# An MoE decoder step on one core: the experts' half tiles move between the raw weights, and they and the weights to rounder addresses

## The reference

```python
def expert_block(args):
    xb, e = args                      # 128 gathered rows, one expert
    hid = jax.nn.silu(xb @ w_gate[e]) * (xb @ w_up[e])
    return hid @ w_down[e]            # 1024 -> 512 -> 1024

yb = lax.map(expert_block, (x_pad, block_e)).reshape(P, D)
```

## The kernel before

| tile | start before | mod 256 |
|---|---|---|
| `raw` (gate, up, down, 16,384 bytes each) | 58,176 | 64 |
| `wh` | 107,328 | 64 |
| `wl` | 156,480 | 64 |
| `xg` | 205,792 | 224 |
| `xh`, `xl` | 209,888 and 213,984 | 224 |
| `hid`, `hh`, `hl` | 218,080, 220,128 and 222,176 | 224 |
| `y` | 224,224 | 224 |

## Time and profile before

### The profile page before, as it was taken

How to read it: one execution, slowest core, us unless ns; L and a number is a source line. 1 busy time by engine, 2 the same in 40 slices (tenths; PEclk the granted TensorE clock), 3 DMA queues, 4 the chain that set the end, 5 groups by cost and what they waited for, 6 DMA issues and landing times. The chain is left out here.

```text
span 2469.8 us, 39160 instructions
## 1 busy us (share of the span) xinstructions
PE 2251.6 (91%) x11590; PEld 1673.2 (68%) x11590; DVE 1330.9 (54%) x2251; ACT 1097.6 (44%) x1870; POOL 326.6 (13%) x387
## 2 busy tenths in 40 slices
PE   7999997889689999999799999999989599999974
PEld 4766665667578888887486565656577488888851
DVE  4223212586766656663683443433367677755757
ACT  3221212642346655663443343434332266645645
POOL 0000002660011111010100433000000010100103
PEclk8999998999889999999899999999999699999987
DMA  7566655655558777785456544333261388866956
GB/s 281 175 209 218 224 190 166 188 178 197 177 206 296 274 251 278 275 292 178 143 169 203 183 147 139 94 103 102 90 214 43 134 319 317 315 230 222 321 196 225
DMA packets 194323, 503.98 MB, mean 204 GB/s; under 512 B 19152, under 2 KB 39089, under 8 KB 187696
## 3 DMA queue, kind: packets, MB, share of 16 engines
q1 hardware_dynamic: 165902, 409.88, 49.0%
q0 software_dynamic: 18416, 64.11, 7.5%
q10 hardware_dynamic: 9906, 28.75, 3.1%
HBM read 437.13 MB, written 73.42 MB: 207 GB/s over the span
## 5 line engine op out<-in xcount | busy, mean ns | idle before, releaser
L2260 DVE TENSOR_TENSOR e_wl<-e_raw,e_wh 128x1024 fp32r<-128x1024 f32 x384 | 452.2, 1221 | 117.2 <-ACT e_wh L2168 116.6
L2168 ACT CAST e_wh<-e_raw 128x1024 fp32r<-128x1024 f32 x384 | 379.4, 1048 | 84.7 <-DMA e_raw<-in_e_up 29.1
L2080 PE MATMUL e_psG<-e_wh,e_xh 128*128 128x512 f32 x784 | 320.5, 409 | 11.5 <-issue 7.4
L2082 PE MATMUL e_psG<-e_wh,e_xl 128*128 128x512 f32 x784 | 310.5, 396 | 0.0
L2081 PE MATMUL e_psG<-e_wl,e_xh 128*128 128x512 f32 x784 | 308.9, 394 | 0.0
L2080 PEld LDWEIGHTS e_psG<-e_wh,e_xh 128*128 128x128 f32 x784 | 147.8, 189 | 45.1 <-issue 12.9
L2082 PEld LDWEIGHTS e_psG<-e_wh,e_xl 128*128 128x128 f32 x784 | 147.4, 188 | 36.8
L2081 PEld LDWEIGHTS e_psG<-e_wl,e_xh 128*128 128x128 f32 x784 | 148.1, 189 | 31.4
L615 PE MATMUL in_ps<-in_w_upper,in_h_upper 128*128 128x512 f32 x384 | 155.3, 404 | 3.3 <-DVE in_h_lower L335 2.9
L2080 PE MATMUL e_psY<-e_wh,e_hh 128*128 128x512 f32 x392 | 155.6, 397 | 2.8 <-DVE e_hl L2283 2.8
L2082 PE MATMUL e_psY<-e_wh,e_hl 128*128 128x512 f32 x392 | 157.1, 401 | 0.0
(11 more groups left out here) (614 smaller groups left out, 4359.1 us busy)
## 6 DMA issues: line engine op xcount, KB each, us to landing
e_raw<-in_e_gate SPq DMA_DIRECT2D x32, 2048.0 KB, 11.7
e_raw<-in_e_up SPq DMA_DIRECT2D x32, 2048.0 KB, 9.1
e_raw<-in_e_down SPq DMA_DIRECT2D x32, 2048.0 KB, 8.1
x<-in_ada_w SPq DMA_DIRECT2D x40, 1024.0 KB, 5.3
yrows<-e_y ACTq DMA_DIRECT2D x49, 512.0 KB, 6.3
x<-in_cache SPq DMA_DIRECT2D x64, 320.0 KB
a_pages<-in_cache SPq DMA_DIRECT2D x64, 320.0 KB, 3.5
qkvo<-in_out SPq DMA_DIRECT2D x48, 256.0 KB, 2.3
```

The source lines that it names most:

```text
L2080: T.matmul(out, upper[:, k, :], wh[:, z, cols], start=k == 0, stop=False)
L2082: mm = T.matmul(out, lower[:, k, :], wh[:, z, cols], start=False, stop=k == PIECES * n - 1)
L2168: S.copy(wh[:, z, c * PC:(c + 1) * PC], raw[:, z, c * PC:(c + 1) * PC]).then_inc(s_hi[z], 1)
L2260: V.tensor_tensor(wl[:, z, at], raw[:, z, at], wh[:, z, at].bitcast(F32), ALU.subtract).then_inc(s_lo[z], 1)
```

## The change

`raw` is taken apart. Gate and up stay where they were; behind them a filler brings the next tile to a multiple of 256 bytes; then come the halves of the gathered rows and of the activations and `hid`, then the raw down weights, then `wh` and `wl`. `xg` and `y` remain last.

```diff
         raw_at = -(-nc.sbuf_base // 32) * 32
-        raw = sb("raw", [P, 3, UNIT])
+        raw_gate_up = sb("raw_gate_up", [P, 2, UNIT])
+        sb("aligning", [P, -nc.sbuf_base % 256 // 4])
+        xh, xl = sb("xh", [P, KD, P], F32R), sb("xl", [P, KD, P], F32R)
+        hh, hl = sb("hh", [P, FT, P], F32R), sb("hl", [P, FT, P], F32R)
+        hid = sb("hid", [P, FE])
+        raw_down = sb("raw_down", [P, UNIT])
+        raw = [raw_gate_up[:, 0, :], raw_gate_up[:, 1, :], raw_down[:]]
         wh = sb("wh", [P, 3, UNIT], F32R)
         routing_at = nc.sbuf_base + UNIT * 4
         wl = sb("wl", [P, 3, UNIT], F32R)
         tokens, tok = sb("tokens", [P, SLOTS], I32), sb("tok", [P, 1], I32)
         xg = sb("xg", [P, D])
-        xh, xl = sb("xh", [P, KD, P], F32R), sb("xl", [P, KD, P], F32R)
-        hid = sb("hid", [P, FE])
-        hh, hl = sb("hh", [P, FT, P], F32R), sb("hl", [P, FT, P], F32R)
         y = sb("y", [P, D])
```

More of the change, by code:

```diff
@@ L2003, in fetch @@
                 src = (g.e_gate, g.e_up, g.e_down)[z]
-                sp.dma_start(raw[:, z, :].rearrange("p (k f) -> p k f", k=KD if z < 2 else FT),
+                sp.dma_start(raw[z].rearrange("p (k f) -> p k f", k=KD if z < 2 else FT),
                              src[bass.ds(e, 1)].rearrange("o (k p) f -> p (o k) f", p=P)).then_inc(s_raw[z], 16)
@@ L2167, in upper @@
                 for c in pieces:
-                    S.copy(wh[:, z, c * PC:(c + 1) * PC], raw[:, z, c * PC:(c + 1) * PC]).then_inc(s_hi[z], 1)
+                    S.copy(wh[:, z, c * PC:(c + 1) * PC], raw[z][:, c * PC:(c + 1) * PC]).then_inc(s_hi[z], 1)
             def renew(z, b, fresh, used, pieces=range(PIECES)):
@@ L2259, in lower @@
                     at = slice(c * PC, (c + 1) * PC)
-                    V.tensor_tensor(wl[:, z, at], raw[:, z, at], wh[:, z, at].bitcast(F32), ALU.subtract
+                    V.tensor_tensor(wl[:, z, at], raw[z][:, at], wh[:, z, at].bitcast(F32), ALU.subtract
                                     ).then_inc(s_lo[z], 1)
```

## The result

| | before | changed |
|---|---|---|
| median | 2472.43 us (five runs, 2470.29 to 2478.13) | 2453.76 us (five runs, 2448.17 to 2462.01) |
| ratio, 95% interval | | 0.9923 [0.9903, 0.9943] |
| profiled execution | span 2469.8 us | span 2448.8 us, its own time 2450.45 us |

The change makes the kernel 0.8% faster: 18.7 us between the medians, where 15.9 were forecast. The time forecast, 2456.3 us, is 2.5 us above the one measured. The interval of the ratio stands for 14 to 24 us, so the times alone don't show that 15.9 was too little; only the traces can say which term was off.

The account below looks back on a forecast made before the run. TensorE bounds both expert stages, so each nanosecond per matmul counts: 19.6 us from faster pitch less 3.7 us lost to late loads gives 15.9 us, 2472.15 to 2456.3 us; range 2450 to 2468 us.

Parts of the forecast that it names:

- The mechanism: Expert matmuls: operands whose starts don't match run at 233.3 ns; matching them as in the front stage gives 226.8 ns.
- the rest from 64: Expert matmuls: mismatch told by starts modulo 64 bytes, moving weights at a multiple, stationary halves 32 bytes past one.
- The rival that nothing happens: Expert matmuls: the slow pitch has another reason, time stays at 2472.15 us within 0.2%; chance 0.12.
- turnings that cost the same at odd and at even places: Turnings of gathered rows, mismatched, have median 272 ns against 273 for aligned attention turnings; cited for no effect.
- The main term: Expert stages: 3528 matmuls at 226.8 ns, 6.5 ns less each when steady; 0.40 us a slot, 19.6 us over 49 slots.
- the slow beginning: Expert groups of 36 matmuls: the first ten after the turning take 2.43 us, so they don't start at the steady pitch.
- Casts, subtractions and the raw down weights: ScalarE, VectorE and down loads in the expert stages: new places change nothing, priced at zero in either direction.
- the 3.7 us of saving lost where the loads pace: Five expert stretches ending in TensorE stalls, 169 us or 9.3 slots: savings of 0.40 us a slot lost, perhaps twice that.
- the load doesn't hear of it: Late weight loads in the experts: from issue to the stall TensorE's saving doesn't reach the load and is lost.
- Slower: Expert weight loads held up by writes into neighbouring tiles outgrow 39 ns of cover; 2479 to 2507 us; chance 0.05.

Follow-up runs that it names:

- e2: Changed kernel's tile order, weights at multiples of 256 bytes, but half tiles and hidden activations 32 bytes past a multiple of 64; 2470.36 us, ratio 0.9999 to the kernel before.
- e4: Changed kernel with the weight halves alone moved 32 bytes on; 2471.40 us, ratio 1.0004 to the kernel before.
- e12: Changed kernel with only the lower half tiles `xl` and `hl` moved 32 bytes on; one run, 2467.74 us.
- e3: Kernel before with weight halves and half tiles all 32 bytes past a multiple of 64; 2458.56 us, ratio 0.9947 to the kernel before.
- e1: Kernel before with a 32-byte filler ahead of the gathered rows, bringing the half tiles to a multiple of 256; 2459.94 us, ratio 0.9956 to the kernel before.
- e10: Changed kernel with all four half tiles 16 bytes past a multiple of 256; one run, 2456.68 us (before: 2472.71).
- e5: Changed kernel with the raw down weights back at 64 bytes past a multiple of 256; 2450.47 us, ratio 0.9917 to the kernel before.
- e8: Changed kernel with the weight halves moved 128 bytes on; one run, 2463.36 us (before, batch median: 2473.34).
- e7: Changed kernel repeated unaltered in the second batch; 2453.28 us, ratio 0.9928 to the kernel before.
- e9: Changed kernel with GpSimd's copy and drain for the next gather behind the wait for the turning; 2458.58 us, ratio 0.9941 to the kernel before.
- e6: Changed kernel with every large expert tile at a multiple of 256, raw gate/up and gathered rows too; 2453.60 us, ratio 0.9927 to the kernel before.
- e11: Changed kernel with the weight halves moved 64 bytes on; one run, 2463.42 us.

## Why the prediction was right, and what was off

**The mechanism is right.** The pitch of the triple is set by how the two operands stand to each other. e2 separates it from the new order of the tiles, e4 and e12 from one special operand, e3 from the alignment of each operand by itself. What was too coarse is how the forecast told the mismatch, by the rest from 64: e1 has both operands at multiples of 64 and gets 4.3 of the 6.6 ns. That the change went all the way to the same rest from 256, as in the front stage, is why its price held. Nor do whole lines of 64 or 32 bytes fit: by them the expectation of e10 had 16 bytes cost as much as 32, and they cost nothing in most groups. Why the differences of 0, 64 and the others have just these pitches no run tells. The rival that nothing happens fell with the result. What spoke for it, turnings that cost the same at odd and at even places, doesn't carry over to the triple; no run tells why. The forecast had that rival supported by the Trainium skill, SBUF — State Buffer, Specifications: lines of 16 bytes would make an offset of 32 harmless. The runs don't agree for 32 bytes, 233.3 ns against 226.7.

**The main term is right in size.** 0.40 us a slot and 19.6 us in all were forecast. The median slots differ by 18.11 - 17.72 = 0.39 us, 19.3 us over 49. Its parts hold too: pitch 226.7 ns, groups of 8.28 and 8.30 us for 8.3, slots of 17.7, medians of 389 ns, the slow beginning kept.

**Casts, subtractions and the raw down weights: nothing, as forecast.** ScalarE's casts take 1046 and 1051 ns, VectorE's subtractions 1223 and 1219, and e5 puts the down loads' target back without a loss. From the page of the changed kernel:

```profile
L2263 DVE TENSOR_TENSOR e_wl<-e_raw_gate_up,e_wh 128x1024 fp32r<-128x1024 f32 x256 | 299.7, 1223 | 97.3 <-ACT e_wh L2171 96.5
...
L2171 ACT CAST e_wh<-e_raw_gate_up 128x1024 fp32r<-128x1024 f32 x256 | 251.2, 1046 | 80.0 <-DMA e_raw_gate_up<-in_e_up 25.3
```

**The term that was mis-sized: the 3.7 us of saving lost where the loads pace.** The step assumed that "the load doesn't hear of it", so that a load issued at the same distance lands at the same distance and every saved 0.4 us comes back as a stall. Measured, lost time went from 2.07 to 2.88 us in the first pair of traces, and from 3.82 to 3.71 with the last slots counted. Over the four traces with the changed timing its mean is 1.85 us, over before, e2, e4, e8 and e12 with slots near 18.1 us it is 1.54; with the last slots 2.26 and 2.06. So the term is 0.2 to 0.3 us instead of 3.7. The loads landed sooner: from the issue of a late up load to ScalarE's first cast behind it (14 loads in a trace, without each stage's first) 13.07 us passed on average before, 12.61 in the changed kernel and 12.2 to 12.4 in e5 to e7. The other kernels with slots near 18.1 us lie at 12.65 to 12.94, so a part of the first pair's difference is the spread between traces; the means of the two groups are 12.85 and 12.39 us.

The loss that was feared exists, though. e9 has the changed kernel's slots and loses 5.63 us, with 13.2 us from issue to cast; e10 loses 7.30 with 13.0, some 1.6 of it in its seven slow groups. So 3.7 us was a price that this stage can take. That the changed kernel doesn't pay it was nothing that the forecast foresaw.

With 19.3 us from the slots and at most 0.8 us lost, by whichever count, 18.5 to 19.4 us are accounted for; the two stages of the traces are 18.9 us shorter, the median moved by 18.7 us, and by 20.1 in e7's batch. The interval of the ratio alone is 10 us wide, so the times can't tell these sizes of the lost term apart.

**"Slower" didn't occur.** Weight loads take 188 ns between tiles that the loads fill.

**What stays open** is why the late loads land sooner in the changed kernel. Two theories were tried. The load's target address fell with e5 and e6. The other started from GpSimd. Its gather's instruction is short or long by how much of a subtraction of VectorE's is still to come when it starts. Before the change, timeline of GpSimd and of VectorE:

```profile
886.98 1.91 POOL L2048 DMA_INDIRECT e_xg<-h,e_tok  x1 [9.09 <-PE e_psX L2072]
...
886.83 1.22 DVE L2260 TENSOR_TENSOR e_wl<-e_raw,e_wh 128x1024 fp32r<-128x1024 f32 x1
```

and the same gather in the changed kernel:

```profile
879.85 0.97 POOL L2051 DMA_INDIRECT e_xg<-h,e_tok  x1 [7.37 <-PE e_psX L2075]
...
879.85 1.26 DVE L2263 TENSOR_TENSOR e_wl<-e_raw_gate_up,e_wh 128x1024 fp32r<-128x1024 f32 x1
```

Before, the subtraction begins 0.15 us ahead of the gather, and the gather ends 0.84 us behind the subtraction's end (888.89 against 888.05). In the changed kernel the two begin together at 879.85; the gather takes 0.97 us, and the subtraction 0.04 us more than before. The median over 47 gathers fell from 1792 to 967 ns, their sum from 71.0 to 52.0 us, which is 19.0 of GpSimd's 21.2 us. If short gathers made the loads faster, e9 would have kept the gain, for its gathers are short as well (median 1052 ns), and it lost it. (The edit was meant to make more of them long and didn't.) What e9 points to is that the time at which the gather comes in the slot matters for how late the loads are: put 0.5 to 1 us later in the slot, behind the store instead of ahead of it, it costs some 4 us (5.63 us of lost time in its one trace against a mean of 1.85 and at most 2.88; the ratios, 0.9941 against 0.9923 and 0.9928, agree with that, though their intervals overlap). The stores of the output tile are issued where they were, but land sooner. The list of DMA issues of the changed kernel (KB, and median us from issue to landing):

```profile
yrows<-e_y ACTq DMA_DIRECT2D x49, 512.0 KB, 6.7
```

and in the view of e9 by tile `y`:

```profile
DMA to landing us min/median/max: 2.6/3.9/9.5
```

In e1, e3, e9 and e10 the stores land in 3.8 to 4.6 us and 3.7 to 7.3 us are lost; in the others they land in 6.2 to 7.3 us and 1 to 2.9 are lost. With the last slots counted the two sets no longer part cleanly: e3 loses 4.20 us and e11, whose stores land in 6.2, loses 4.80. So it is a hint and no proof: which transfer gives way to which on the DMA engines wasn't measured by itself.

## What to carry to other kernels

When the same triple of matmuls has different pitches in two stages, compare where their stationary and moving tiles start: bring both to the same rest from 256 bytes, since with a difference of 64 only two thirds of the gain in pitch came (4.3 of 6.6 ns), and in time 0.9956 and 0.9947 against 0.9923. An allocator that rounds tiles to 32 bytes can lose 3% of such a matmul without any sign in the waits. And in a stage that TensorE and the loads both nearly fill, moving one small transfer by a microsecond seems to be worth some 4 us, as much as one nanosecond per matmul (3.5 us here), so stalls must be read anew after each change.

## What the runs showed of the hardware

- **The pitch depends on the difference of the operands' starts.** A difference of 0 gives 226.7 ns, 240 (16 bytes apart) the same in 85 of 92 groups, 64 gives 229.0, 32, 96 and 224 give 233.3, and 128 gives 232.3 and 233.3 on average, in an irregular pattern. The weight load's own 188 ns doesn't change. The Trainium skill, SBUF — State Buffer, Who interferes with whom, gives TensorE independent ports for the moving operand and for the weights, and has it wait for nobody; here the relative place of just these two costs 6.6 ns of 226.7.
- **One odd load in three costs as much as three** (e12: distances of 233, 239 and 228 ns, 233.3 on average).
- **16 bytes of distance remove the slower stretch at a group's beginning.** Most groups of e10 go at 226.6 ns from their second start; their first ten starts take 2.35 us, where with a difference of 0 they take 2.38. The first distance, 0.31 us, is in both.
- **The gather's instruction on GpSimd waits for a VectorE subtraction** with both inputs in SBUF that is under way: it takes 0.97 us when the two begin together and 1.91 when the subtraction is 0.15 us ahead, and then ends 0.84 us behind the subtraction. That agrees with the Trainium skill, same page and section, by which a VectorE instruction with two inputs in SBUF contends with a GpSimd instruction that reads SBUF.
